# Two transformer blocks in one kernel: row norms without a diagonal matrix, down projections ended bank by bank, and a later reading of the conditioning matrix

## What is computed

```
mod = silu(c) @ ada_w[i] + ada_b[i]            # c: 1024 numbers, ada_w[i]: 1024 x 6144
sh1, sc1, g1, sh2, sc2, g2 = split(mod, 6)
h = rms_norm(x, norm_mix[i]) * (1 + sc1) + sh1
x = x + g1 * mix(h)      # i = 0: stick-breaking attention, 16 heads; i = 1: latent attention with a top-128 index
h = rms_norm(x, norm_ffn[i]) * (1 + sc2) + sh2
x = x + g2 * conv_ffn(h) # up to 2 x 2816, causal conv of width 3, silu(gate)*val, down
```

## Time and profile before

| | us |
|---|---|
| median of 3 runs | 2167.24 |
| lowest, highest | 2165.22, 2168.67 |
| the profiled execution, its own time | 2167.39 |
| its span, first to last instruction | 2165.6 |
| PE busy (the page, part 1) | 2034.1, 94% of the span |
| DVE, ACT, POOL busy | 1034.0 (48%), 603.3 (28%), 1215.7 (56%) |

### The profile page before, as it was taken

The page is one execution under the profiler, slowest core; times in us unless marked ns, Lnnn a source line. Parts: engine busy times, 40 slices in busy tenths (PEclk is TensorE's granted clock), DMA queues, the critical chain, the costliest instruction groups (busy, mean ns, idle before and its releaser), DMA issues.

```text
span 2165.6 us, 26887 instructions
## 1 busy us (share of the span) xinstructions
PE 2034.1 (94%) x9346; PEld 1624.7 (75%) x9346; DVE 1034.0 (48%) x1611; ACT 603.3 (28%) x1134; POOL 1215.7 (56%) x678
## 2 busy tenths in 40 slices
PE   5999799997998899899899999999999998999999
PEld 4876678886887677666788888878686577888887
DVE  4456469989225800365443333131784744333422
ACT  2226210000113320597231111121316823111210
POOL 6650568886663766433566666654352046666664
PEclk9999889999998899999999999988999999999999
DMA  6330258887231222100423333321121012333331
GB/s 232 127 117 1 78 172 287 287 286 248 87 97 49 78 97 92 45 1 0 156 78 97 97 97 93 95 84 49 60 77 40 1 55 73 97 97 97 97 97 68
DMA packets 62327, 221.15 MB, mean 102 GB/s; under 512 B 6913, under 2 KB 7169, under 8 KB 62129
## 3 DMA queue, kind: packets, MB, share of 16 engines
q1 hardware_dynamic: 44928, 161.25, 23.4%
q10 hardware_dynamic: 17328, 58.95, 7.7%
HBM read 218.03 MB, written 2.14 MB: 102 GB/s over the span
## 4 chain that ended last, share of the span: by engine, by line
PE 62%; ACT 6%; DVE 6%; issue 2%; DMA 0%; POOL 0%; ACTq 0%; DVEq 0%
PE bank L280 17%; PE bank L281 17%; PE bank L282 17%; PE bank L310 1%; PE bank L315 1%; PE bank L311 1%; PE bank L588 1%; ACT y L658 1%; ACT L666 1%; PE bank L381 1%; PE bank L450 1%; PE bank L475 1%; DVE big L1530 1%; ACT tmp L515 1%; ACT tmp L521 1%
## 5 line engine op out<-in xcount | busy, mean ns | idle before, releaser
L280 PE MATMUL bank<-a_hi,w_hi 128*128 128x512 f32 x2072 | 813.3, 393 | 10.3 <-DVE a_lo L812 4.9
L282 PE MATMUL bank<-a_hi,w_lo 128*128 128x512 f32 x2072 | 808.5, 390 | 0.0
L281 PE MATMUL bank<-a_lo,w_hi 128*128 128x512 f32 x2072 | 808.5, 390 | 0.0
L857 POOL TENSOR_SCALAR w_hi<-raw 128x1024 fp32r<-128x1024 f32 x299 | 356.9, 1194 | 755.7 <-PE bank L282 496.0
L859 POOL TENSOR_TENSOR w_lo<-raw,w_hi 128x1024 fp32r<-128x1024 f32 x299 | 764.9, 2558 | 24.9
L280 PEld LDWEIGHTS bank<-a_hi,w_hi 128*128 128x128 f32 x2072 | 390.4, 188 | 94.1 <-POOL w_lo L859 5.5
L282 PEld LDWEIGHTS bank<-a_hi,w_lo 128*128 128x128 f32 x2072 | 390.3, 188 | 81.9
L281 PEld LDWEIGHTS bank<-a_lo,w_hi 128*128 128x128 f32 x2072 | 390.5, 188 | 81.2 <-issue 0.7
L1334 DVE CUSTOM_DVE_ANT_0 y<-y,cond 128x1024 f32<-128x1024 f32 x96 | 212.7, 2267 | 0.5 <-DMA y<-in_ada 0.5
L1345 DVE SCALAR_TENSOR_TENSOR tmp<-bank,vecs,tmp 128x511 f32<-128x511 f32 x88 | 66.0, 750 | 263.1 <-ACT tmp L1093 263.1
L1093 ACT ACTIVATE tmp<-bank,vecs 128x512 f32<-128x512 f32 x88 | 68.5, 781 | 372.2 <-PE bank L282 364.6
(11 more groups left out here) (207 smaller groups left out, 2307.2 us busy)
## 6 DMA issues: line engine op xcount, KB each, us to landing
raw<-in_stream SPq DMA_DIRECT2D x299, 512.0 KB, 3.5
y<-in_ada ACTq DMA_DIRECT2D x96, 512.0 KB, 4.7
x<-in_x SPq DMA_DIRECT2D x4, 512.0 KB, 7.1
bias<-in_bias ACTq DMA_DIRECT2D x1, 2048.0 KB, 14.1
y<-rel_rows ACTq DMA_DIRECT2D x1, 2048.0 KB, 9.4
bias<-rel_rows ACTq DMA_DIRECT2D x1, 2048.0 KB, 14.2
out<-x SPq DMA_DIRECT2D x8, 256.0 KB, 2.1
cond<-in_c ACTq DMA_DIRECT2D x1, 512.0 KB, 9.2
```

The lines of the kernel that those rows point to most:

```text
L280: pe.matmul(o, lhs_hi, rhs_hi, start=start, stop=False, **kw)
L281: pe.matmul(o, lhs_hi, rhs_lo, start=False, stop=False, **kw)
L282: return pe.matmul(o, lhs_lo, rhs_hi, start=False, stop=stop, **kw)
L857: pool.tensor_scalar(w_hi[:, s, :], raw[:, j, :], 1.0, 1.0, ALU.mult, ALU.mult).then_inc(high_ready, 1)
```

## The change

Norms: `dve_write_diag`, its tensor and its counters go. PE waits for the last step of `dve_inverse` and makes four matmuls of 128 columns each, with the column of 1/rms spread over the stationary matrix and the identity as the moving one.

Down projections: the blocks 20 and 21 are worked through bank by bank, six matmuls for a bank, and both blocks' slots come free at the very end. Three sum groups instead of two are put between the banks.

POOL splits two blocks (AHEAD) instead of four ahead of the six norms' low parts; the other two come behind them.

Conditioning: three columns behind each tile's product in gu1 (counted in ADA_TURN; three and four in the last turn), and the last 21 one by one in down1, each behind the low part of a hidden chunk. ACT issues their loads there ahead of each a_hi. The bias and the gains are made behind the low parts of pe_gate. The first eight columns go straight into mods.

```diff
 MOD = 6 * DC
 SPAN = 640
 ADA_STEP = 8
+ADA_TURN = 12
+ADA_LAST = (range(68, 71), range(71, 75))
+AHEAD = 2
 PHASES = [("z", 4), ("u", 4), ("q", 4), ("k", 4), ("v", 4), ("out1", 8), ("gu1", 2 * FC), ("down1", FC),
...
+        def pe_spread_rows(pe):
+            for t in range(TT):
+                m = pe.matmul(rstd_bank[:, t * P:(t + 1) * P], rms[:, 1, t:t + 1].broadcast_to([P, P]), ident, start=True, stop=True)
+            return m
         def pe_spread(pe, name):
-            pe.wait_ge(diag_ready, NORM_INDEX[name] + 1)
-            pe.matmul(rstd_bank[:], ones, diag[:].rearrange("p t i -> p (t i)"), start=True, stop=True).then_inc(rstd_ready, 1)
+            pe.wait_ge(inverse_step, 5 * inverse_index(name) + 5)
+            pe_spread_rows(pe).then_inc(rstd_ready, 1)
...
                     m = pe_three_passes(pe, bank[c][:], w_hi[:, s, c * P:(c + 1) * P], w_lo[:, s, c * P:(c + 1) * P],
-                                        hi, lo, start, stop, skip_group_check=True)
-                    if stop and c < DC - 1:
-                        m.then_inc(down_done, 1)
-                    elif c == (3 if start else DC - 1):
+                                        hi, lo, start, False, skip_group_check=True)
+                    if c == (3 if start else DC - 1):
                         m.then_inc(block_done, 1)
-                    if stop and norm and c in (5, 7):
-                        pe_sum_group(pe, norm, c // 2 - 2)
             for j in range(4):
                 chunk(j, j, start=j == 0)
             with pe.Fori(1, FC // 4) as r:
                 for j in range(4):
                     chunk(j, r * 4 + j)
-            for i in range(FC // 4 * 4, FC):
-                chunk(i % 4, i, stop=i == FC - 1)
+            last = range(FC // 4 * 4, FC)
+            for i in last:
+                pe.wait_ge(split_ready, START[name] + 1 + i)
+                pe.wait_ge(lo_ready, LOW_AT[name] + 1 + i)
+            for c in range(DC):
+                for i in last:
+                    s, j = (START[name] + i) % SPLIT, i % 4
+                    m = pe_three_passes(pe, bank[c][:], w_hi[:, s, c * P:(c + 1) * P], w_lo[:, s, c * P:(c + 1) * P],
+                                        a_hi[:, j, :], a_lo[:, j, :], False, i == FC - 1, skip_group_check=True)
+                    if c == DC - 1:
+                        m.then_inc(block_done, 1)
+                if c < DC - 1:
+                    m.then_inc(down_done, 1)
+                if norm and c in (3, 5, 7):
+                    pe_sum_group(pe, norm, c // 2 - 1)
...
                 dve_add_squares(v, name)
             v.wait_ge(group_used, GROUP_AT[name] + len(NORM_GROUPS[name]))
             dve_inverse(v, rms, sum_columns(name), P * NORM_CHUNKS[name], (rms_ready, s + 1), inverse_index(name))
-            dve_write_diag(v).then_inc(diag_ready, 1)
             if wait:
                 v.wait_ge(rstd_ready, s + 1)
...
-        def dve_write_diag(v):
-            return v.tensor_tensor(diag[:], ident.unsqueeze(1).broadcast_to([P, TT, P]),
-                                   rms[:, 1, :].unsqueeze(2).broadcast_to([P, TT, P]), ALU.mult)
...
                     a.wait_ge(hidden_ready, 2 + FC * (name == "down3") + t + 1)
+                if name == "down1":
+                    n = ADA_LAST[1][-1] + t
+                    a.wait_ge(ada_done, n - 3)
+                    ada_load(a, n, n % 4)
                 a.activation(a_hi[:, t % 4, :], big[:, t, :], ACT.Copy).then_inc(hi_ready, 1)
         def dve_split_hidden(v, name):
...
                 v.wait_ge(hi_ready, SPLIT_AT[name] + t + 1)
                 v.tensor_tensor(a_lo[:, t % 4, :], big[:, t, :], f32(a_hi[:, t % 4, :]), ALU.subtract).then_inc(lo_ready, 1)
+                if name == "down1":
+                    dve_ada_column(v, ADA_LAST[1][-1] + t)
         def wait_down(e, n, c):
...
             pool.wait_ge(zeroed, 2)
-            for b in range(SPLIT):
+            for b in range(AHEAD):
                 split(b, b, b, 0, wait=False)
             pool_lows("pre_mix")
-            split_stream(SPLIT, START["gu1"] + SPLIT)
+            for b in range(AHEAD, SPLIT):
+                split(b, b, b, 0, wait=False)
+            split_stream(SPLIT, START["gu1"] + AHEAD)
             pool_lows("pre_ffn")
-            split_stream(START["gu1"] + SPLIT, START["bq"] + SPLIT)
+            split_stream(START["gu1"] + AHEAD, START["bq"] + AHEAD)
             pool.wait_ge(x_ready, X_AT["pe_gate"] + DC)
-            pool.wait_ge(split_ready, START["bq"] + SPLIT)
+            pool.wait_ge(split_ready, START["bq"] + AHEAD)
             pool.memset(big[64:P, 0:B_HEADS:2, :], 0.0).then_inc(zeroed, 1)
             pool.wait_ge(zeroed, 3)
             pool.memset(big[0:64, 1:B_HEADS:2, :], 0.0).then_inc(zeroed, 1)
             pool.wait_ge(zeroed, 4)
             pool_lows("mix0")
-            split_stream(START["bq"] + SPLIT, START["out2"] + SPLIT)
+            split_stream(START["bq"] + AHEAD, START["out2"] + SPLIT)
             for h in range(B_HEADS):
...
-            def silu_turn(r, split=False):
-                for jj in range(2):
-                    for m in range(4):
-                        a.wait_ge(ada_done, r * ADA_STEP + (ADA_STEP + 4 * jj + m - 3))
-                        ada_load(a, r * ADA_STEP + (ADA_STEP + 4 * jj + m), m)
-                    a.wait_ge(block_done, START["gu1"] + 2 * jj + 1 + 4 * r)
-                    a.activation(tmp[:, 2 * jj, :], bank[2 * jj][:], ACT.Silu).then_inc(silu_ready, 1)
-                    if split and jj == 0:
-                        act_split_first_hidden(a, "down1")
-            with a.Fori(0, FC // 2 - 1) as r:
-                silu_turn(r)
-            silu_turn(FC // 2 - 1, split=True)
+            def silu_tile(jj, block, loads):
+                for n in loads:
+                    a.wait_ge(ada_done, n[0] - 3)
+                    ada_load(a, *n)
+                a.wait_ge(block_done, block)
+                a.activation(tmp[:, 2 * jj, :], bank[2 * jj][:], ACT.Silu).then_inc(silu_ready, 1)
+            with a.Fori(0, FC // 4) as r:
+                for turn in range(2):
+                    for jj in range(2):
+                        q = 6 * turn + 3 * jj
+                        silu_tile(jj, START["gu1"] + 4 * turn + 2 * jj + 1 + 8 * r,
+                                  [(r * ADA_TURN + (ADA_STEP + n), n % 4) for n in range(q, q + 3)])
+            for jj in range(2):
+                silu_tile(jj, START["gu1"] + 2 * (FC - 2 + jj) + 1, [(n, n % 4) for n in ADA_LAST[jj]])
+                if jj == 0:
+                    act_split_first_hidden(a, "down1")
             act_split_hidden(a, "down1")
             a.wait_ge(p_landed, 16)
...
-        def dve_ada(v, n, m, part):
+        def dve_ada(v, m, column):
             w = y_flat[:, m * D:(m + 1) * D]
-            v.tensor_tensor_reduce(w, w, cond[:], 1.0, 0.0, ALU.mult, ALU.add, ada_part[:, part:part + 1]).then_inc(ada_done, 1)
+            v.tensor_tensor_reduce(w, w, cond[:], 1.0, 0.0, ALU.mult, ALU.add, column).then_inc(ada_done, 1)
+        def dve_ada_column(v, n):
+            v.wait_ge(ada_landed[n % 4], 16 * (n // 4 + 1))
+            dve_ada(v, n % 4, mods[:, n:n + 1])
         def dve_conv(v, layer):
...
             for n in range(ADA_STEP):
-                v.wait_ge(ada_landed[n % 4], 16 * (n // 4 + 1))
-                dve_ada(v, n, n % 4, n)
-            v.wait_ge(ada_done, ADA_STEP)
-            v.tensor_copy(mods[:, 0:ADA_STEP], ada_part[:]).then_inc(ada_copied, 1)
+                dve_ada_column(v, n)
             dve_diag(v, "sgu", wait=False)
...
-            def product_turn(r, split=False):
-                for jj in range(2):
-                    v.wait_ge(silu_ready, jj + 1 + 2 * r)
-                    v.wait_ge(block_done, START["gu1"] + 2 * jj + 2 + 4 * r)
-                    v.tensor_tensor(big[:, bass.ds(r * 2 + jj, 1), :].rearrange("p o s -> p (o s)"), tmp[:, 2 * jj, :],
-                                    bank[2 * jj + 1][:], ALU.mult).then_inc(banks_free["dve"], 2)
-                    if split and jj == 0:
-                        dve_split_first_hidden(v, "down1")
-                    for m in range(4):
-                        v.wait_ge(ada_landed[m], r * 32 + 16 * (3 + jj))
-                        if jj == 0 and m == 0:
-                            v.wait_ge(ada_copied, r + 1)
-                        dve_ada(v, None, m, 4 * jj + m)
-                v.wait_ge(ada_done, r * ADA_STEP + 2 * ADA_STEP)
-                v.tensor_copy(mods[:, bass.ds(r * ADA_STEP + ADA_STEP, ADA_STEP)], ada_part[:]).then_inc(ada_copied, 1)
-            with v.Fori(0, FC // 2 - 1) as r:
-                product_turn(r)
-            product_turn(FC // 2 - 1, split=True)
-            v.wait_ge(ada_copied, 2 * MOD // ADA_STEP)
-            v.tensor_tensor(mods[:], mods[:], vec("ada_b_2", 0, 2 * MOD), ALU.add).then_inc(mods_ready, 1)
-            v.wait_ge(mods_ready, 1)
-            for n in range(4):
```

(37 more changed lines are left out.)

29 lines of the change are left out of this document (16 added, 13 removed).

## The result

| | before | after |
|---|---|---|
| median of the runs shown together (4 each), us | 2167.95 | 2138.38 |
| lowest, highest | 2165.22, 2168.92 | 2136.64, 2140.95 |
| ratio, 95% interval | | 0.9867, 0.9849 to 0.9884 |
| the profiled execution, and its span | 2167.39, 2165.6 | 2140.95, 2139.1 |
| PE, DVE busy | 2034.1, 1034.0 | 2030.6, 978.2 |

The kernel is 29.6 us faster; the forecast was 27.2, and a time of 2140. A second series of the changed kernel gave 2135.87 (2134.86 to 2144.35, 6 runs). Over both series the ten runs have the median 2136.7; six lie between 2134.86 and 2136.80 and four between 2139.96 and 2144.35, both profiled executions among the four.

The account below looks back on a forecast made before the run. PE, busy 94% of the span, bounds the kernel, so only its waits and slow stretches can give time. Norms 6.2, POOL's order 6.3, down 7.1 and conditioning 7.6 sum to 27.2 us off 2167.39: 2140, range 2132 to 2150.

Parts of the forecast that it names:

- the spread's +0.15: In each norm, eight 128-column matmuls instead of two of 512 were taken to cost 0.15 us more.
- The cover at post_ffn: PE has other matmuls ahead of the spread there, so no gain; 0.6 us if that cover went.
- The range of -10 to 7.5: Bounds in us put on the 6.2 us gain from all norms together.
- In the first norm 2.73 + 0.04 less 0.15: 2.6: First norm: dropping the diagonal and its wait, less the spread's extra cost, gains 2.6 us.
- POOL's 3.5: First norm: chunk 1's low part no longer waits for two splits, 2.5 us, plus 1.0 from fewer slow matmuls.
- The 2.6 before mix0: DVE's last two steps before mix0, 1.25 and 2.71 us beside a split, fall to 0.7 each: 2.6 us gained.
- The 0.9 for the third block: Loss from splitting the third block behind the low parts: 0.7 us in mix0, 0.2 at four other norms together.
- Down1's 4.7: Down1's new bank order: inverse begins 3.5 us earlier, pe_proj matmuls behind it may run faster; 3.5 to 5.9, taken 4.7.
- The 2.4 of down2: Down2's bank order with three sum groups between banks ends the sums 2.4 us earlier.
- Rival C: Down projections: square, sum and inverse behind the last bank set the norm, so no gain there, 2147; chance 0.08.
- The bounds of 1.8 and 9.5: Gain limits in us for the seam's 7.6: four columns all at 3.35 us, or all at 1.22.
- Rivals B and D: B: seam's columns all at 3.35 us, 2146, chance 0.15; D: down1's columns stretch POOL's splits past PE's pace, to 2176, 0.03.

Follow-up runs that it names:

- u_down: Changed kernel with the down projections' last two blocks back in the old order, block by block with two sum groups between: 2142.76 us.
- u_ada: Changed kernel with all 88 columns back in gu1, and copy, bias and gains ahead of chunk 1's low part: 2145.06 us.
- down1_only: Changed kernel with the bank order kept in down1 alone, down2 and down3 block by block again: 2137.96 us.
- u_pool: Changed kernel with POOL again splitting four blocks instead of two ahead of the low parts at all six norms: 2150.14 us.

## Why the prediction was right, and where its steps were not

The forecast's case held: 2138.4 (or 2136.7) for 2140, inside 2132 to 2150. Stage by stage, gain forecast and seen in the profiled executions: up to the second projection 6.1 and 6.8 (54.61 less 47.82); from there to post_mix 0 and a loss of 3.1 (stages with the same code in other kernels are 1.4 shorter each, the clock's share; 0.3 has no row); pre_ffn 1.7 and 2.4; gu1, seam and down1 11.7 and 12.0; mix0 3.8 and 5.3 (1.4 to 1.7 longer in u_down, u_ada and down1_only with the same code there, so the surplus is the clock's too); ffn0 -0.1 and 1.3; mix1 3.0 and 2.2; the rest 1.2 and -0.3. Together 27.2, with the small debits of the third blocks, and 26.5.

- **The norm.** Right as a whole, 6.4 by the chains for 6.2, and 4.1 to 8.4 by the medians; the spread's +0.15 was 0.08 in the slow case (2.19 against 2.11 from spread to scaling). The cover at post_ffn went in part, which adds the 0.6 that the prediction named for that case. The range of -10 to 7.5 doesn't follow from the prediction's own terms, which give -8.2 to 7.2. At full clock the narrow spread costs PE itself more, start to start of the next matmul 0.81 against 0.46, in the norm attn, here before and after:

```profile
210.50 1.02 PE L388 MATMUL bank<-diag,consts 128*128 128x512 f32 x2
210.96 0.79 PE L310 MATMUL bank<-a_hi,w_hi 128*128 128x512 f32 x1
```

```profile
206.83 1.05 PE L390 MATMUL bank<-consts,rms 128*128 128x128 f32 x8
207.64 0.48 PE L312 MATMUL bank<-a_hi,w_hi 128*128 128x512 f32 x1
```

The rule of the Trainium skill, "TensorE: Matmul & The Clock Gate", section "LDWEIGHTS (loading the stationary operand)", would have six more loads at 0.64 us, an estimate from its 107 ns a load. The trace has 0.35 at full clock for PE's next matmul, so a little under half of them is hidden, and 0.08 for the scaling that waits.

- **POOL's order.** The step that failed is "In the first norm 2.73 + 0.04 less 0.15: 2.6", put beside POOL's 3.5 as if either stood alone. The sum of both was right, the shares weren't: undone alone, POOL's order takes the diagonal's gain with it. The 2.6 before mix0 (seen 2.9) and the 1.1 of post_mix (seen 1.1) held. The 0.9 for the third block was wrong, nothing waits (a reading of the traces; no run tests it by time).
- **Down.** Down1's 4.7 came out in after (3.86 up to the inverse and 1.43 behind it, where pe_proj's matmuls keep the full clock), but that the clock holds was in part luck: down1_only has 2.65 and nothing behind it. Against the gain stands the 2.25 us step at 649.23, for which PE waits 0.66 and which the prediction did not see: it counted only that the slots come free later, not that their splits then fall on the inverse. The 2.4 of down2 failed: I moved sums that PE makes in either order, and the time there was the splits beside the additions. Rival C holds in down2, not in down1.
- **The seam.** 7.6 forecast, 7.45 by the stage of u_ada. Chunk 1 begins 11.6 us after gu1's last matmul (18.8 in the kernel before), forecast 11.2: the four columns take 8.0 (515.84 to 523.81), forecast 4 x 2.1, and the low part 2.81, somewhat over its bound of 2.2. The bounds of 1.8 and 9.5 don't come out of its own terms: from 523.0, four columns at 1.22 and a low part of 1.0 end at 528.9, a gain of 12.0, and at 3.35 and 2.2 at 538.6, a gain of 2.3. The 7.45 lies within either. Rivals B and D didn't come: `w_lo` 2690 against 2662 ns.

Alone, the four parts are worth 33.7 us against 2136.7 (27.0 against 2138.4), the change 31.3 (29.6). They don't add up exactly, for reasons shown above: the first norm's 2.6 counts twice and the 2.2 us step of mix1 exists in u_pool alone, while down2's 2 us count in none of the four. With these three put right the 33.7 become 30.9, close to 31.3. From the first series it would be 24.2 for 29.6: an error of the base counts four times in such a sum, so it can't prove the account.

## What to carry to other kernels

Two edits at one wait are not two terms: ask of each what it is worth with the other undone, since they may need each other (the diagonal behind POOL's splits) or replace each other (the splits beside the additions). Where two engines block each other, a transfer or split that is freed later lands on something else; look at what stands there. And work that nobody waits for goes behind the first low part of the next phase, not ahead of it: the last four columns were worth 6 to 8 us more.
